# Padding and another order of SBUF buffers, so that TensorE's operands start at multiples of 128 bytes

## What is computed

```python
def swiglu(h, w_up, w_down):
    gate, up = jnp.split(h @ w_up, 2, axis=-1)      # 1024 -> 2 x 2816
    return (jax.nn.silu(gate) * up) @ w_down        # 2816 -> 1024

for layer in range(2):
    h = rms_norm(x, g[0])
    x = x + 0.5 * rms_norm(swiglu(h, w_ffn_in[layer, 0], w_ffn_out[layer, 0]), g[1])
    proj = rms_norm(x, g[2]) @ w_in[layer]
    qa, ka, va, qh, fh, ih, gh = jnp.split(proj, splits, axis=-1)
    ya = rms_norm(sliding_window_sink_attention(qa, ka, va, ...), attn_out_gain[layer])
    yh = hgrn2_mixer(qh, fh, ih, gh, ...)
    x = x + rms_norm(jnp.concatenate([ya, yh], axis=-1) @ w_out[layer], g[3])
    h = rms_norm(x, g[4])
    x = x + 0.5 * rms_norm(swiglu(h, w_ffn_in[layer, 1], w_ffn_out[layer, 1]), g[5])
```

## Time and profile before

| | |
|---|---|
| Time, median of 3 runs | 1933.62 us (1932.35 to 1933.71) |
| The profiled execution's own time | 1933.36 us |
| Its span, first to last instruction | 1931.4 us |
| Mean granted clock of TensorE | 0.996 of full speed (2.4 GHz) |
| TensorE matmul busy | 1909.9 us, 99% of the span, 11434 matmuls |
| VectorE, ScalarE, GpSimd busy | 678.2, 726.6, 809.7 us (35%, 38%, 42%) |
| Moved by DMA | 182.77 MB, 95 GB/s in the mean |

### The profile page before, as it was taken

How to read it: one execution, slowest core, us unless ns; L and a number is a source line. 1 busy time by engine, 2 the same in 40 slices (tenths; PEclk the granted TensorE clock), 3 DMA queues, 4 the chain that set the end, 5 groups by cost and what they waited for, 6 DMA issues and landing times.

```text
span 1931.4 us, 29831 instructions
## 1 busy us (share of the span) xinstructions
PE 1909.9 (99%) x11434; PEld 1586.2 (82%) x11434; DVE 678.2 (35%) x1147; ACT 726.6 (38%) x1115; POOL 809.7 (42%) x367
## 2 busy tenths in 40 slices
PE   9999999999999999999999999999999999999997
PEld 7888888877878888888888888888788788888887
DVE  4222210376765322211162222005676562222103
ACT  5232222456645322232352232324565553232321
POOL 4444354333235334344434344453333344444452
PEclk9999999999999999999999999999999999999999
DMA  6322233221112222232222222232211122322231
GB/s 198 106 90 98 98 109 109 88 99 57 66 66 95 91 97 93 102 109 98 99 88 98 98 90 105 99 109 88 99 67 56 66 99 87 109 87 103 95 113 60
DMA packets 54335, 182.77 MB, mean 95 GB/s; under 512 B 6728, under 2 KB 10472, under 8 KB 54248
## 3 DMA queue, kind: packets, MB, share of 16 engines
q1 hardware_dynamic: 54248, 181.52, 27.2%
HBM read 179.01 MB, written 2.49 MB: 94 GB/s over the span
## 4 chain that ended last, share of the span: by engine, by line
PE 96%; DVE 1%; ACT 1%; DVEq 1%; DMA 0%; SPq 0%; issue 0%; ACTq 0%; POOLq 0%; POOL 0%
PE bank L793 26%; PE bank L795 25%; PE bank L794 25%; PE bank L822 3%; PE bank L814 3%; PE bank L815 3%; PE pair L795 2%; PE pair L793 2%; PE pair L794 2%; PE pair L970 2%; PE pair L842 1%; PE bank L1041 0%; DMA RAW<-stream 0%; PE pair L1030 0%; PE pair L1088 0%; PE pair L1003 0%
## 5 line engine op out<-in xcount | busy, mean ns | idle before, releaser
L411 POOL TENSOR_TENSOR WLO<-RAW,WHI 128x1024 fp32r<-128x1024 f32 (+1 forms) x334 | 789.9, 2385 | 1095.4 <-ACT WHI L480 1024.9
L794 PE MATMUL bank<-HLO,WHI 128*128 128x512 f32 (+1 forms) x1536 | 595.5, 388 | 0.0
L793 PE MATMUL bank<-HHI,WHI 128*128 128x512 f32 x1472 | 579.6, 394 | 0.0
L795 PE MATMUL bank<-HHI,WLO 128*128 128x512 f32 x1472 | 574.1, 390 | 0.0
L480 ACT ACTIVATE WHI<-RAW 128x1024 fp32r<-128x1024 f32 (+1 forms) x334 | 335.7, 1038 | 87.7 <-PE bank L795 55.1
L794 PEld LDWEIGHTS bank<-HLO,WHI 128*128 128x128 f32 x1536 | 289.2, 188 | 58.5 <-issue 0.5
L793 PEld LDWEIGHTS bank<-HHI,WHI 128*128 128x128 f32 x1472 | 277.0, 188 | 57.9 <-issue 0.5
L795 PEld LDWEIGHTS bank<-HHI,WLO 128*128 128x128 f32 x1472 | 277.0, 188 | 57.9
L793 PE MATMUL bank<-UHI,WHI 128*128 128x512 f32 x616 | 242.7, 394 | 0.0
L795 PE MATMUL bank<-UHI,WLO 128*128 128x512 f32 x616 | 241.5, 392 | 0.0
L794 PE MATMUL bank<-ULO,WHI 128*128 128x512 f32 x616 | 239.0, 388 | 0.0
(11 more groups left out here) (231 smaller groups left out, 1967.9 us busy)
## 6 DMA issues: line engine op xcount, KB each, us to landing
RAW<-stream SPq DMA_DIRECT2D x335, 512.0 KB, 3.2
yT<-X SPq DMA_DIRECT2D x16, 128.0 KB, 1.7
X<-xT SPq DMA_DIRECT2D x3, 512.0 KB, 7.9
RAW<-stream SPq DMA_DIRECT2D x2, 256.0 KB, 3.3
X<-xT SPq DMA_DIRECT2D x2, 256.0 KB, 4.2
bias<-rel_scratch SPq DMA_DIRECT2D x4, 128.0 KB
rel_scratch<-SM SPq DMA_DIRECT2D x1, 382.0 KB
mask_sb<-masks SPq DMA_DIRECT2D x1, 128.0 KB, 8.4
```

The lines of the kernel that those rows point to most:

```text
L411: pool.tensor_tensor(WLO[:, n, 0:cols], RAW[:, n, 0:cols], WHI[:, n, 0:cols], ALU.subtract)\
L793: pe.matmul(dst, WHI[:, slot, lhs], rhs_hi, start=first, stop=False)
L794: pe.matmul(dst, WHI[:, slot, lhs], rhs_lo, start=False, stop=False)
L795: ins = pe.matmul(dst, WLO[:, slot, lhs], rhs_hi, start=False, stop=last)
```

## The change

```diff
+PAD = 16
...
         small = sb("small", [P, 3, 8])


+        sb("to_line", [P, PAD])
         with ExitStack() as ffn_scope:
             UHI = sb("UHI", [P, FT, SEQ], F32R, ffn_scope)
             ULO = sb("ULO", [P, FT, SEQ], F32R, ffn_scope)
+        ZHI = sb("ZHI", [P, KT, SEQ], F32R)
         kT = sb("kT", [P, CHUNK + SEQ])
         vT = sb("vT", [P, CHUNK + SEQ])
         vwin = sb("vwin", [P, 8, P])
         SM = sb("SM", [P, 2 * HCHUNKS, LOCAL])
         SMB = sb("SMB", [P, 2 * HCHUNKS, LOCAL])
-        S = sb("S", [P, 8 * WINDOW + 8])
         PT = sb("PT", [P, 8, P])
...
         QE = sb("QE", [P, 2, SEQ])
-        TREE_F = sb("TREE_F", [P, TREE[NLEV]])
         KHT = sb("KHT", [P, HCHUNKS, P])
...
         YSQ = sb("YSQ", [P, SEQ])
         RP = sb("RP", [P, SEQ])
-        ZHI = sb("ZHI", [P, KT, SEQ], F32R)
+        TREE_F = sb("TREE_F", [P, TREE[NLEV]])
+        S = sb("S", [P, 8 * WINDOW + 8])
```

## The result

The changed kernel takes **1941.43 us** (median of 6 runs, 1939.59 to 1942.42) against 1933.39 us before: a ratio of 1.0041 with a 95% interval of 1.0031 to 1.0051. It is slower, by 8.0 us, where 1929.5 us had been forecast. It lies above the range, on the side of rival D.

What follows compares the result with a forecast made beforehand. TensorE's time per matmul was taken to bound the kernel; -4.1 (down), -1.2 (out), +1.0 and +0.2 (halves) summed to -4.1 us, giving 1929.5 us, range 1926.9 to 1933.0.

Steps and rivals of the forecast that it cites:

- rival D: Operands' phase to the weights by 512 bytes counts; down slows to 235.0 ns, 11.3 us more, 1944.9 us; chance 0.07.
- What bounds the kernel: Whole kernel: TensorE's matmuls fill 99% of the span, so its time per matmul is the kernel's time.
- the pace of rows 3: Gate and up, operands `HHI` and `HLO`: 192 matmuls in 43.52 us, 226.67 ns each, taken over for down.
- The term of -4.1 us: Down, 512 columns: 1848 matmuls go from 228.89 to 226.67 ns each, saving 4.1 us.
- the three paces: 226.7, 228.9 and 235.0 ns per 512-column matmul, said to go with starts 0, 64 and 96 bytes past a multiple of 128.
- The output projection: Mixer's out stage, 512 columns: matmuls with `ZHI` and triples get faster, -1.2 us; triples reach 680.0 ns.
- The halves: Matmuls of 256 columns slow towards 120.0 ns: +1.0 us in down, +0.2 us in out.
- fixed step: Streams with operands at multiples of 128 settle into one pitch, shorter at 512 columns, longer at 256 (120.0 ns).
- The mixer's small matmuls: Mixer's float32 sums and `chunk` pieces: place does not show, 0 us; at most 1.6 us either way for the pieces.
- VectorE, 0,: VectorE's writes take 692 ns at 64 and 691 ns at a multiple of 128, so no price.
- Rivals B and C: B: multiples of 64 suffice, only `ZHI` gains, 1932.6 us, chance 0.15. C: place has no effect, 1933.6 us, chance 0.08.
- the mixer's starts: Slow start of the mixer's 48 `chunk` pieces after interruptions, 33 ns each; taken as 0, half better in the 1927 case.

Runs made afterwards that it cites:

- The first run: Kernel before the change, with each FFN's hidden activations at its own place: 0, 128, 256, 384 bytes past the weights by 512; 1936.50 us against 1932.92.
- the last run: Kernel before the change, with one of two hidden activations per FFN out of phase with the weights (FFN 3: the high one by 192 bytes); 1935.91 us.

## Why the prediction was wrong

- **What bounds the kernel** held. TensorE's pitch is the kernel's time: 4 x 2.03 us in down are the loss, and moving the two weight buffers by 128 bytes cost 26 us with no instruction and no wait changed.
- **"I take the pace of rows 3 for all: they are the same three lines of the program with operands that lie where `UHI` and `ULO` will lie."** This is the step that failed. The term of -4.1 us was +8.1. The reading that the three paces go with the start by 128 bytes was an ordering of three points, 0, 64 and 96, that went together with another one: the distance to the weights, 0, 64 and 96 by 256. The first run and the one with moved weights take the two apart. `HHI` lies at a multiple of 128, but what gave it 226.7 ns is that it lies a multiple of 256 from `WHI` and `WLO`; `UHI` was moved to a distance of 128. With the padding of 192 bytes the four downs came to 4 x 1.05 = 4.2 us under before, the size that the term had.
- **The output projection**, -1.2 us: the same step, 0.2 us less for its 512 and 256 columns together. With the distance right the triples came to the 680.0 ns of the forecast.
- **The halves**, +1.2 us in sum, hung on the same step. At the distance 0 they take 119.9 ns, as the earlier trace rows had said; in the changed kernel they took 118.6. The sentence that a stream with its operands at multiples of 128 falls into a fixed step has the same fault: with all of them 64 bytes past one the pitch is 226.7 as well.
- **The mixer's small matmuls, 0,** and **VectorE, 0,** held: a full float32 pass from `YSQ` has a mean of 632 ns (631 before), the write of `ULO` 692 ns as in the earlier trace rows.
- **Rival D** was the right one: the place that counts is another, relative to the weights, with the pitch in down as the sign, over 231. It was priced from the pace of `ZHI` at 235.0 ns and 1944.9 us; 233.3 and 1941.4 came. Its period, put at 512, is 256 bytes. The argument held against it, that 64 and 96 "are ordered by how far they break a line", was no evidence: the table shows no such order, 64 is a good place between two bad ones.
- **Rivals B and C** fall: nothing of either shows once the distance is 0.
- The rule of 16-byte lines that the prediction weighed (the Trainium skill, SBUF — State Buffer, section Specifications (TRN2)) does not explain the paces: every place in the table is a multiple of 32, and they differ by up to 7.6 ns.
- Two slips in the working changed nothing. With the halves at their other end and the mixer's starts half better the terms give 1926.4, not some 1927. And the earlier trace rows show VectorE and ScalarE lighter in down than in gate and up, but GpSimd a little heavier (46% against 43%), and the transfers too (0.32 against 0.28).

## What to carry to other kernels

An address has more than one reading: before "aligned" is taken for the cause, put the distance to the other operand of the same engine beside it, since one padding ahead of a buffer changes both at once. Where TensorE streams float32r against weights that change with each matmul, in calls of 512 columns, try moving operands at a multiple of 256 bytes from the weight buffers and look at the pitch in the timeline; here one padding of 192 instead of 64 bytes was the difference between 1941.4 and 1928.7 us. Several places can be tried in one execution if a stage occurs several times.

## What was not expected of the hardware

The pitch of a matmul hangs on how far its moving operand lies from the weights. The Trainium skill (TensorE: Matmul & The Clock Gate, section Step-by-step: what each phase is for) gives TensorE two independent read ports of SBUF and says that loading the next tile's weights does not steal bandwidth from the running matmul. Measured, moving the weights by 128 bytes away from `HHI` and `HLO` took gate and up from 226.7 to 232.3 ns per matmul, and the slow pace stays where no other engine works; the measurement decides. That the load and the stream get in each other's way is the reading that is left; how they do it no run shows.

Many of the losses come in steps. Triples took 680.0, 686.7, 693.3 or 700.0 ns in the mean in many of the places tried (3 x 226.67, 228.9, 231.1, 233.3), that is 680 and a number of steps of 6.7 ns, which at the granted 2.4 GHz are 16 clocks. This is a pattern of the means and no rule: at the distance of 128 single triples change between 0.71 and 0.69 us, as the rows from 897.69 on show, and 697.1 with the weights moved, 696.7 and 699 with `ZHI` at 96 and at 64, 702.8 at 160 and 703.2 in FFN 3 of the last run are off the grid. And the best place depends on the width: at 256 columns the distance of 192 bytes was fastest, 113.5 ns, and 0, the best at 512, among the slowest, 119.9.
